# Mixture-of-experts loop: one pass per expert, six weight halves in one ring, and a body of its own for experts of up to 32 rows

## What is computed

```python
logits = hf @ router_w + router_b                  # 256 tokens, 32 experts
top_val, top_idx = lax.top_k(logits, 4)
top_w = softmax(top_val)
for e in range(32):                                # rows: the tokens that chose e
    g = minimum(xs @ w_gate[e] + b_gate[e], 7)
    u = clip(xs @ w_up[e] + b_up[e], -7, 7)
    act = g * sigmoid(1.702 * g) * (u + 1)
    y[rows] += (act @ w_down[e] + b_down[e]) * row_w
```

## Time and profile before

| | us |
|---|---|
| median of 3 runs | 2554.79 |
| lowest, highest | 2546.99, 2555.33 |
| span of the profiled execution | 2552.7 |
| PE busy in it | 2212.0 (87%) |
| DVE, ACT busy | 651.7, 357.1 |
| expert loop, first gate product to closing rows | 442.06 to 1437.61 |

### The profile page before, as it was taken

One profiled execution on the slowest core, in us unless ns is written; L12 is line 12 of the kernel. 1 busy time (PEld: TensorE's weight loads), 2 busy tenths in 40 slices (PEclk: granted clock), 3 DMA queues, 4 the chain that ended last, 5 costly groups with the idle time before them and its releaser, 6 DMA issues.

```text
span 2552.7 us, 24185 instructions
## 1 busy us (share of the span) xinstructions
PE 2212.0 (87%) x9951; PEld 1237.3 (48%) x9952; DVE 651.7 (26%) x997; ACT 357.1 (14%) x548; POOL 103.9 (4%) x116
## 2 busy tenths in 40 slices
PE   6977789998899999999999797799979686858997
PEld 2643346333333333333333384488548475837873
DVE  2747623110111111111111115100016465420000
...
GB/s 346 207 230 50 66 192 204 398 428 359 263 427 428 427 428 428 428 262 413 428 427 417 290 163 65 83 151 146 133 130 132 99 1 1 1 67 116 139 109 17
DMA packets 106791, 580.77 MB, mean 228 GB/s; under 512 B 6992, under 2 KB 8084, under 8 KB 81969
## 3 DMA queue, kind: packets, MB, share of 16 engines
...
## 4 chain that ended last, share of the span: by engine, by line
PE 67%; DMA 16%; DVE 11%; ACT 3%; issue 2%; SPq 0%; DVEq 0%; POOL 0%; ACTq 0%
DMA ring<-in_w_up 14%; PE ps L1199 14%; PE ps L1586 12%; PE ps L1597 6%; PE ps L604 6%; PE ps L612 5%; PE ps L1214 5%; PE ps L516 1%; PE ps L1931 1%; PE ps L1222 1%; PE ps L1937 1%; DMA ring<-in_ada_w 1%; PE ps L825 1%; PE ps L1941 1%; PE ps L793 1%
## 5 line engine op out<-in xcount | busy, mean ns | idle before, releaser
L1199 PE MATMUL ps<-ring,arena 128*64 128x512 f32 x1632 | 362.6, 598 | 29.5 <-DMA ring<-in_w_up 23.5
L1586 PE MATMUL ps<-arena,ring 128*128 128x256 f32 x1408 | 308.2, 382 | 1.5 <-ACT arena L581 1.5
L1586 PEld LDWEIGHTS ps<-arena,ring 128*128 128x128 f32 x1408 | 270.0, 192 | 39.6 <-ACT arena L581 2.3
L1214 PE MATMUL ps<-ring,arena 128*64 128x512 f32 x1088 | 240.9, 594 | 9.0 <-ACT arena L1161 9.0
L1199 PEld LDWEIGHTS ps<-ring,arena 128*64 128x64 f32 x1632 | 114.7, 138 | 271.7 <-issue 231.2
L1134 DVE TENSOR_SCALAR arena<-ps 128x512 f32<-128x512 f32 x34 | 23.5, 692 | 546.3 <-PE ps L1199 546.3
L1214 PEld LDWEIGHTS ps<-ring,arena 128*64 128x64 f32 x1088 | 88.3, 137 | 139.1 <-issue 138.3
L1597 PE MATMUL ps<-ring,arena 128*128 128x512 f32 x352 | 151.4, 592 | 0.0
L604 PE MATMUL ps<-arena,ring 128*128 128x256 f32 x672 | 149.1, 384 | 0.7 <-ACT arena L581 0.7
L604 PEld LDWEIGHTS ps<-arena,ring 128*128 128x128 f32 x672 | 129.1, 193 | 20.4 <-issue 1.5
L1199 PE MATMUL ps<-arena 128*64 128x512 f32 x544 | 124.5, 611 | 11.2 <-issue 11.2
...
## 6 DMA issues: line engine op xcount, KB each, us to landing
ring<-in_w_up SPq DMA_DIRECT2D x64, 2048.0 KB, 17.3
ring<-in_w_down SPq DMA_DIRECT2D x64, 2048.0 KB, 16.2
ring<-in_w_gate SPq DMA_DIRECT2D x32, 2048.0 KB, 15.9
arena<-in_w_gate SPq DMA_DIRECT2D x32, 2048.0 KB, 15.9
ring<-in_ffn_w_gate_up SPq DMA_DIRECT2D x22, 2048.0 KB, 7.9
ring<-in_ada_w SPq DMA_DIRECT2D x12, 2048.0 KB, 17.7
ring<-in_ffn_w_down SPq DMA_DIRECT2D x10, 2048.0 KB, 7.7
ring<-in_w_in SPq DMA_DIRECT2D x8, 2048.0 KB, 18.0
```

Source lines behind the costliest of these rows:

```text
L1199: m = pe.matmul(bank(b)[c * CAP:(c + 1) * CAP, :], xT[:, j * P + h * CAP:j * P + (h + 1) * CAP], w[h][:, j, c * 512:(c + 1) * 512], start= ...
L1214: m = pe.matmul(bank(b)[d * CAP:(d + 1) * CAP, :], actT[:, j * P + h * CAP:j * P + (h + 1) * CAP], down_w[h][:, j, d * 512:(d + 1) * 512], ...
L1586: m = pe.matmul(bank(b0 + g)[:, c * SEQ:(c + 1) * SEQ], w[:, k, (2 * g + c) * P:(2 * g + c + 1) * P], hT2[:, k, :], start=(k == 0), stop=( ...
```

## The change

One pass of the loop is one expert (`Fori(0, E)`), and the body is chosen by two branches: up to FEW = 32 rows (`few`), up to 64 (`narrow`), more (`wide`, now one copy). The few body holds 32 rows as weights, so that four products (gate and up, two column halves each) stand side by side in 32-column tiles of one bank; in down the four tiles are two column halves by two halves of the matrix, and combine adds the two partial sums, since `Pw` then holds each row's weight twice (`both`, `far`). The bias is opened at the start of a body from a selector `E32` or `E64` and a bias table of 4 x 32 rows. The transposes of `Pw` lie between the halves of the products and are the expert's own, not the next one's.

The six ring slots hold the six halves of one expert in the order gate 0, up 0, gate 1, up 1, down 0, down 1. `g_ps`, `u_ps` and `d_ps` are told once per half, and SP asks for each half of expert e + 1 when its own slot is free. The two arena places are gone. Behind the loop SP goes on with the next layer's pieces as their slots come free.

```diff
         W7 = [RING[:, i * SLOT_W:(i + 1) * SLOT_W] for i in E_SLOT]
-        gate_w = [[x.rearrange("p (k n) -> p k n", k=4) for x in xs] for xs in (W7[0:2], odd_gate)]
-        up_w = [W7[2 + h].rearrange("p (k n) -> p k n", k=4) for h in range(2)]
-        down_w = [W7[4 + h].rearrange("p (k n) -> p k n", k=4) for h in range(2)]
+        gate_w, up_w, down_w = ([W7[i].rearrange("p (k n) -> p k n", k=4) for i in of] for of in ((0, 2), (1, 3), (4, 5)))
...
+        def dve_weights(dve, s, e, r):
+
+            for t in range(TT):
+                if r == 0:
+                    dve.tensor_scalar(Pm, slot_iota(0, 2 * CAP), posm[:, t, bass.ds(e, 1)], None, ALU.is_equal)
+                    dve.drain()
+                    dve.scalar_tensor_tensor(Pm, slot_iota(0, 2 * CAP), both[:, t, bass.ds(e, 1)], Pm, ALU.is_equal, ALU.add)
+                    dve.drain()
+                    m = dve.tensor_scalar(Pw[:, t, :], Pm, wt[:, t, bass.ds(e, 1)], None, ALU.mult)
+                else:
+                    m = dve.tensor_scalar(Pw[:, t, :], slot_iota(r, 2 * CAP), posm[:, t, bass.ds(e, 1)], wt[:, t, bass.ds(e, 1)],
+                                          ALU.is_equal, ALU.mult)
                 if t == 0:
                     dve.drain()
             m.then_inc(s.pw_ready, 1)
 
-        def dve_glu(dve, s, n, g_at, u_at, banks=(0, 1)):
+        def dve_bias_of(dve, e):
+
+            dve.tensor_scalar(E32.rearrange("p (q n) -> p q n", q=4), cols_bc(con("quarters"), FEW),
+                              con("pick4")[:, bass.ds(e, 1)], None, ALU.mult)
+            dve.tensor_scalar(E64.rearrange("p (q n) -> p q n", q=2), cols_bc(con("halves"), CAP),
+                              con("pick4")[:, bass.ds(e, 1)], None, ALU.mult).then_inc(main.e_ready, 1)
...
+        def pe_product(pe, w, h, xT, b, done):
+
+            for j in range(4):
+                for c in range(2):
+                    m = pe.matmul(bank(b)[c * CAP:(c + 1) * CAP, :], xT[:, j * P + h * CAP:j * P + (h + 1) * CAP],
+                                  w[h][:, j, c * 512:(c + 1) * 512], start=False, stop=(h + j == 4), skip_group_check=True)
+            if done is not None:
+                m.then_inc(done, 1)
+
+        def pe_hidden(pe, s, n, b, of):
             pe.wait_ge(s.a_ready, n * 2)
             for j in range(4):
-                m = pe.transpose(bank(0)[:, j * P:(j + 1) * P], every4(act_, j), ident)
+                m = pe.transpose(bank(b)[:, j * P:(j + 1) * P], every4(of, j), ident)
             m.then_inc(s.aT_ps, 1)
 
...
+        def pe_few(pe, e, there):
             n = e + 1
             pe.wait_ge(main.x_ready, n * 2)
-            there(0)
-            pe_product(pe, gate_w[odd], XT, 0, main.g_ps)
-            there(1)
-            pe_product(pe, up_w, XT, 1, main.u_ps)
+            pe.wait_ge(main.e_ready, n)
+            pe.matmul(bank(0), E32, bgu, start=True, stop=False, skip_group_check=True)
+            for h in range(2):
+                there("g", h)
+                there("u", h)
+                for j in range(4):
+                    for i, (w, done) in enumerate(((gate_w, main.g_ps), (up_w, main.u_ps))):
+                        for c in range(2):
+                            m = pe.matmul(bank(0)[(2 * i + c) * FEW:(2 * i + c + 1) * FEW, :],
+                                          XT[:, j * P + h * CAP:j * P + h * CAP + FEW], w[h][:, j, c * 512:(c + 1) * 512],
+                                          start=False, stop=(h + j == 4), tile_position=(0, (2 * i + c) * FEW), skip_group_check=True)
+                        if j == 3:
+                            m.then_inc(done, 1)
+                if h == 0:
+                    pe_weights(pe, main, n)
 ...
             pe_gather(pe, main, n + 1)
-            pe.wait_ge(main.a_ready, n * 2 - 1)
-            pe_weights(pe, main, n + 1)
-            pe_hidden(pe, main, n)
+            pe.wait_ge(main.pwT_ready, n)
+            pe.wait_ge(main.a_ready, n * 2)
             pe_gatherT(pe, main, n * 2 + 1)
-            there(2)
-            pe_down(pe, main, n, 2, main.d_ps)
-            pe.wait_ge(main.pwT_ready, n + 1)
-            pe_open(pe, 0, 1 - odd, 0)
-            pe_open(pe, 1, 1 - odd, 1)
-            pe_combine(pe, main, n, PwT[odd])
-
-        def act_narrow(act, e, odd):
+            for j in range(4):
+                m = pe.transpose(bank(0)[:, j * CAP:(j + 1) * CAP], every4(act_[0:CAP, :], j), ident[0:CAP, 0:CAP])
+            m.then_inc(main.aT_ps, 1)
+            there("d", 0)
+            there("d", 1)
+            pe.wait_ge(main.aT_ready, n)
+            for j in range(4):
+                for d in range(2):
+                    for h in range(2):
+                        g = 2 * d + h
+                        m = pe.matmul(bank(2)[g * FEW:(g + 1) * FEW, :], actT[:, j * CAP + h * FEW:j * CAP + (h + 1) * FEW],
+                                      down_w[h][:, j, d * 512:(d + 1) * 512], start=(j == 0), stop=(j == 3), tile_position=(0, g * FEW))
+                        if (j, d) == (3, 1):
+                            m.then_inc(main.d_ps, 1)
+            pe_combine(pe, main, n, PwT, Yb)
+
...
+        def act_few(act, e):
             n = e + 1
+            act_weights(act, main, n, PwT)
+            act.wait_ge(main.gm_ready, n)
+            act.activation(sg[0:CAP, :], gm[0:CAP, :], ACT.Sigmoid, scale=ALPHA).then_inc(main.sg_ready, 1)
+            act_gathered(act, main, n * 2 + 1)
+            act_gatheredT(act, main, n * 2 + 2, XT)
+            act.wait_ge(main.aT_ps, n)
+            act.copy(actT[:, 0:4 * CAP], bank(0)[:, 0:4 * CAP]).then_inc(main.aT_ready, 1)
+            act_out(act, main, (main.d_ps, n * 2), 2, Yb)
+
+        def dve_few(dve, e):
+            n = e + 1
+            dve.wait_ge(main.x_ps, e * 2 + 1)
+            dve_weights(dve, main, e, 0)
+            dve_rows(dve, main, e + 1, 0)
+            dve.wait_ge(main.u_ps, n * 2)
+            dve.tensor_scalar(gm[0:CAP, :], bank(0)[0:CAP, :], LIMIT, None, ALU.min).then_inc(main.gm_ready, 1)
+            dve.tensor_scalar(um[0:CAP, :], bank(0)[CAP:2 * CAP, :], LIMIT, -LIMIT, ALU.min, ALU.max).then_inc(main.a_ready, 1)
+            dve.drain()
+            dve.scalar_tensor_tensor(um[0:CAP, :], um[0:CAP, :], 1.0, gm[0:CAP, :], ALU.add, ALU.mult)
+            dve.drain()
+            dve.wait_ge(main.sg_ready, n)
+            dve.tensor_tensor(act_[0:CAP, :], um[0:CAP, :], sg[0:CAP, :], ALU.mult).then_inc(main.a_ready, 1)
+
...
+        def pe_narrow(pe, e, there):
+            n = e + 1
+            pe.wait_ge(main.x_ready, n * 2)
+            pe.wait_ge(main.e_ready, n)
+            pe_open(pe, 0)
+            for h in range(2):
+                there("g", h)
+                pe_product(pe, gate_w, h, XT, 0, main.g_ps)
+                if h == 0:
+                    pe_weights(pe, main, n)
+                there("u", h)
+                pe_product(pe, up_w, h, XT, 1, main.u_ps)
+            pe_gather(pe, main, n + 1)
+            pe.wait_ge(main.pwT_ready, n)
+            pe_gatherT(pe, main, n * 2 + 1)
+            pe_hidden(pe, main, n, 0, act_)
+            there("d", 0)
+            pe.wait_ge(main.aT_ready, n)
+            pe_down(pe, 0, actT, 2, main.d_ps)
+            there("d", 1)
+            pe_down(pe, 1, actT, 2, main.d_ps)
+            pe_combine(pe, main, n, PwT, Yb)
...
+        def pe_wide(pe, e, x, there):
 
             n = e + 1
             pe.wait_ge(main.x_ready, n * 2)
-            there(0)
-            pe_product(pe, gate_w[odd], XT, 0, extra.g_ps)
+            pe.wait_ge(main.e_ready, n)
+            pe_open(pe, 0)
+            there("g", 0)
+            pe_product(pe, gate_w, 0, XT, 0, None)
             pe_gather(pe, extra, x)
-            pe_weights(pe, extra, x, 3)
-            there(1)
-            pe_product(pe, up_w, XT, 1, extra.u_ps)
+            pe_weights(pe, main, n)
+            there("u", 0)
+            pe_product(pe, up_w, 0, XT, 1, None)
+            pe.wait_ge(main.pwT_ready, n)
+            pe_gatherT(pe, extra, x * 2)
+            pe.wait_ge(extra.x_ready, x * 2 + 1)
+            pe_open(pe, 2)
+            pe_product(pe, gate_w, 0, XTf, 2, main.g_ps)
+            pe_product(pe, up_w, 0, XTf, 3, main.u_ps)
+            there("g", 1)
+            pe_product(pe, gate_w, 1, XT, 0, extra.g_ps)
+            pe_product(pe, gate_w, 1, XTf, 2, main.g_ps)
+            there("u", 1)
+            pe_product(pe, up_w, 1, XT, 1, extra.u_ps)
+            pe_product(pe, up_w, 1, XTf, 3, main.u_ps)
+            pe_hidden(pe, main, n, 0, act_)
+            pe_weights(pe, extra, x, 1)
+            there("d", 0)
+            pe.wait_ge(main.aT_ready, n)
+            pe_down(pe, 0, actT, 0, None)
+            pe_hidden(pe, extra, x, 2, actf)
+            pe.wait_ge(extra.aT_ready, x)
+            pe_down(pe, 0, actTf, 3, main.d_ps)
+            there("d", 1)
+            pe_down(pe, 1, actT, 0, extra.d_ps)
+            pe_down(pe, 1, actTf, 3, main.d_ps)
...
```

(49 more changed lines are left out.)

309 lines of the change are left out of this document (131 added, 178 removed).

## The result

The changed kernel takes 2539.04 us (median of four runs, 2536.00 to 2543.74), against 2555.06 for the kernel before on the same chip: a ratio of 0.9941, with a 95% interval of 0.9921 to 0.9961, 0.6% faster. Predicted were 2541.6 and 0.5%. The profiled execution is the longest of the four, with a span of 2542.0.

The account below looks back on a forecast made before the run. The weight transfer was taken to bound the expert loop. Span 2552.7, less 14.2 for the loop, plus 1 for slow clocks, gave 2539.5; the median's 2.1 above span made it 2541.6 us, range 2516 to 2564.

Parts of the forecast that it names:

- Transfer-bound: Expert loop: weight transfer sets the floor, 29.4 us an expert; about 55 us of transfers did not run.
- Few rows: Body for up to 32 rows: 20.2 us an expert, 9.2 under the transfer; makes no transfer faster.
- Narrow 29.9: Body for 33 to 64 rows: 29.9 us, 2.2 more than before and 0.5 over the transfer.
- rival 1: Loop: an instruction fetch at each change of body, 6 us each giving 2584; chance 12%.
- short of that this part costs and gives nothing: Release by halves: no transfer starts late while PE's release lags the landing by less than 24.5 us.
- The walk: Step-by-step timing of the loop: end at 1421, 14.2 us less than the same reckoning for the kernel before.
- The stall at expert 21: Second wide expert: a stall going in and none coming out, as before; the expert costs 20 us in all.
- rival 3: Wide experts run the same code: fewer fetches, the second's 8.2 us fall away, 2533, or 2517 with none; chance 25%.
- Three DVE steps before the loop: Ahead of the loop: three steps of 0.2 us hidden under PE's 3.7 us of bias rows, costing nothing.
- first reload: Loop start: gate 0 is done at 446.7 us and its next transfer moves from 448.3.
- Slow clock, 1 us: Products after starved waits: 1 us taken, 3.4 if every wait of over 3 us costs 2.7.
- Rival 2: Few body: slow clock throughout, products 1.5 times as long, loop end 1432, time 2552, no change; chance 6%.

Follow-up runs that it names:

- clamped pair: The change and the kernel before, each with counts clamped to 64 so that no expert is wide: 2494.29 us for the change, 2489.24 for the kernel before.
- change_again: The change itself, unedited, timed once more against the kernel before: 2541.89 us, ratio 0.9947.
- wide_inside: The change with the wide body's code inside the loop, behind the narrow body, instead of at the program's end: 2534.24 us, ratio 0.9928.
- two_wides: The change with the wide body written twice, experts of index over 15 taking the second copy: 2554.39 us, ratio 0.9996.
- count_first: The change with the counts copied and told ahead of the three new DVE steps: 2536.84 us, ratio 0.9946.
- waits_kept: The change with SP's two waits behind the loop (`ff_ps` and the gains) put back: 2538.66 us, ratio 0.9942.

## Why the prediction was right, and where it was not

**Transfer-bound, and the gain lies round the wide experts.** Right, and shown by the clamped pair. One list in the working is off: PE's time for a narrow expert names the gather's 1.8 us beside 4.0 that already hold it (780.58 to 784.61 in the earlier trace rows), so its items add up to 29.3 and not to the 27.8 that it takes. The sums for both new bodies count it once.

**Few rows make PE faster but no transfer.** Right. The four tiles do run side by side: 32 records in 3.64 us, 0.11 each, 0.10 by the earlier trace rows, so gate and up take 7.3 us for the 6.9 of the sum. The body was put at 20.2 us; where nothing is missing it takes 21.9 (1143.06 to 1164.97). The term that was too small is down, 3.4 in the sum and 5.25 here, at a granted clock of 0.69. Of the 17 downs of this profile 13 took 4.9 to 6.2 us and four 3.64, and change_again has three at 3.64:

```profile
1156.90:1162.20 5.30, 5.25 (x32) 1.27 (x32) 1.63 (x6) 0.00 (x0) 0.00 (x0) 0.69 1.00 430
...
517.66 3.64 PE L1279 MATMUL ps<-ring,arena 128*32 128x512 f32 x32 [0.55 <-ACT arena L1293]
```

**Narrow 29.9, no fetch at a change of body.** 29.6 measured (524.11 to 553.71 to 583.31). PE's waits for issue in the loop of the change come to 11 us, 10.5 of them round expert 6; none stands at a change between few and narrow, so rival 1 is refuted for this layout. wide_inside shows what it rested on: coming round past code not yet run and the first entry to the narrow body cost 6 us there, once each.

**Halves "short of that this part costs and gives nothing".** Right away from the wide experts (the clamped pair), but round them the halves are worth 7 us alone and 8 to 11 in the change. The walk had them in its release times and did not name them as a term of the gain, of which they make about half.

**The stall at expert 21.** Here the forecast failed and rival 3, at 25%, came true: one copy of the wide body, kept together with the loop. The 8.2 us taken for stall and slow clock did not come. The kernel before ran a second copy there, with 5.5 us going in and a slow start. two_wides is not that case over again: its second copy opened after 0.78 us and cost 10.5 on the way back, 12 to 15 in all.

**Three DVE steps before the loop "lie under PE's 3.7 us of bias rows".** Wrong. PE's bias rows wait for `pos_ready`, which those steps delay: 1.71 us of idle for 0.99, then the bias rows at the low level for a part (4.63 for 3.67 us), and the opening (2.08 us for the 1.10 of count_first) and the first products (5.32 for 3.64) too; the gather's 3.7 us were 3.6 before. The first reload was put 446.7 us into the program and is asked for at 452.3. The step that failed is taking the steps as covered by work that was waiting for them. count_first gives 4.0 of these 5.6 us back (14.3 us from the bias rows to the reload for 18.3), and the loop's end moves by less: a delay at the start is not carried to the end whole, as the walk had it.

**Slow clock, 1 us.** At the last expert it alone costs 3.4 (5.41 and 5.22 for 3.64 twice). The prediction had 3.4 as its upper bound, but for waits alone; 1.6 of it is down, which waited for no weights.

**The sum.** The walk gave 1421 for the loop's end, the profiles have 1424.3 and 1420.6. That it comes so near is luck, because the misses cancel: 8.2 us too much for expert 21, 5.6 too little at the start, 2.4 at the end. Walk against walk it gave 14.2 us less for the loop; counted from the bias rows, the two profiles of the change have 15.1 and 18.1. Nothing behind the loop moved, as said: waits_kept is the same time, and attention's first transposes follow the closing rows after 20.1 us in both kernels.

**Clock and code.** In the change, the second half of gate and up, behind waits for weights of 2.42 us and of 4.5 to 5.8 us, ran at the low level for a part: 4.9 to 6.6 us for 3.64, and not the 7.3 of double length. In change_again a wait of 2.27 us cost nothing. Most downs ran slow without a wait for weights. The Trainium skill (TensorE: Matmul & The Clock Gate, HAM oscillation) says that where the wait for data outlasts the burst of matmuls, each burst starts slow; the rows agree with the slow start and give its size here, 1.3 to 3.0 us more on 3.64. Gate and up of a fed expert took 3.64 twice. Rival 2, every product 1.5 times as long, came partly true: gate and up of the few experts took 154.6 us and down 84.1, 1.3 times the 185.6 of 51 halves at 3.64. It cost little, as those experts had time to spare.

In wide_inside three bodies are kept, with no instruction packet from 575 us on. One pass through each is 502 matmul records and as many weight loads, about 1,000 instructions without those that wait or count. The Trainium skill (Advanced Engine Details and Errata, ISA Cache) gives the instruction cache 128 KB on TensorE, where other engines have 32 KB in two lines of 256 instructions. An estimate from that page's figures is eight such lines for TensorE, 2,048 instructions, and the trace agrees that about 1,000 are kept. The loop and both wide copies of two_wides, about 1,500, would fit by the same estimate, and there the trace disagrees: the loop was not kept. What sets that limit is open.
